# A hybrid encoder layer on one core: whole weight blocks, a router on the unnormalised sum, and a reordered end

## The reference, cut to what matters

```python
def rms_norm(x, g):
    y = x * lax.rsqrt(jnp.mean(x * x, axis=-1, keepdims=True) + RMS_EPS)
    return y * g

x = x + einsum('bsd,de->bse', y_rwkv * g, w_out)          # 512 x 1024
h = rms_norm(x, norm_ffn_g)
# expert_choice_moe: 16 experts, each takes cap = 2*512/16 = 64 tokens
logits = einsum('bsd,de->bse', h, router_w)               # 512 x 16
aff = softmax(logits, axis=-1)
gates, idx = lax.top_k(swapaxes(aff, 1, 2), cap)
xin = h[bidx, idx]
hid = silu(xin @ w_gate) * (xin @ w_up)                   # 64 x 2048 per expert
yexp = (hid @ w_down) * gates
x = x + zeros.at[bidx, idx].add(yexp)
out = rms_norm(x, final_norm_g)
```

## Time and profile before

| | before |
|---|---|
| median of 3 runs | 1600.93 us |
| profiled execution | 1600.83 us, span 1599.0 us |
| PE busy | 1461.1 us (91%) |
| DVE busy | 510.5 us (32%) |
| ACT busy | 240.1 us (15%) |
| DMA queue q1 | 479.31 MB, 78.2% of 16 engines' span |
| read from HBM | 470.83 MB |
| mean granted TensorE clock | 0.982 of full speed |

### The profile page before, as it was taken

The page is one execution under the profiler, slowest core; times in us unless marked ns, Lnnn a source line. Parts: engine busy times, 40 slices in busy tenths (PEclk is TensorE's granted clock), DMA queues, the critical chain, the costliest instruction groups (busy, mean ns, idle before and its releaser), DMA issues.

```text
span 1599.0 us, 26196 instructions
## 1 busy us (share of the span) xinstructions
PE 1461.1 (91%) x11376; PEld 735.6 (46%) x11376; DVE 510.5 (32%) x712; ACT 240.1 (15%) x478; POOL 184.5 (12%) x349
## 2 busy tenths in 40 slices
PE   7999999989888895899989989989989989989987
PEld 5344455878877653434324324324324324324322
DVE  6666534667664564101101101101101101101103
ACT  3333321222212121100000000000000000000002
POOL 1323504434333210000000000000000000000000
PEclk9999999999998997899999999999999999999999
DMA  9245577766765645499999999999999999999994
GB/s 302 66 158 185 183 264 161 176 136 133 149 111 127 263 172 210 187 428 425 421 428 422 425 427 426 425 425 427 423 426 426 425 424 428 423 425 427 422 425 184
DMA packets 186070, 500.47 MB, mean 313 GB/s; under 512 B 125904, under 2 KB 135248, under 8 KB 153216
## 3 DMA queue, kind: packets, MB, share of 16 engines
q1 hardware_dynamic: 180192, 479.31, 78.2%
q0 software_dynamic: 5792, 19.88, 3.6%
HBM read 470.83 MB, written 28.33 MB: 312 GB/s over the span
## 4 chain that ended last, share of the span: by engine, by line
PE 32%; DMA 23%; DVE 2%; issue 1%; ACT 1%; DVEq 0%; SPq 0%
DMA ring<-in_exp_w_up 23%; PE pD L1543 14%; PE pG L1504 6%; PE pU L1524 6%; PE pX L1492 4%; PE pG L1524 3%; DVE res L1652 1%; DVE hid L1670 1%; PE pX L1531 1%; ACT hidT L1613 0%; DVE res L1688 0%; ACT xin L1596 0%; PE pX L1560 0%; ACT xin L1628 0%; ACT L1631 0%
## 5 line engine op out<-in xcount | busy, mean ns | idle before, releaser
L1670 DVE TENSOR_TENSOR hid<-silu,pU 128x512 f32<-128x512 f32 x32 | 20.6, 684 | 774.5 <-PE pU L1524 774.5
L1524 PE MATMUL pU<-ring,xin 128*64 128x512 f32 x768 | 173.8, 597 | 37.8 <-DMA ring<-in_exp_w_up 37.8
L1524 PE MATMUL pG<-ring,xin 128*64 128x512 f32 x768 | 171.3, 595 | 11.4 <-DMA ring<-in_exp_w_gate 10.7
L1543 PE MATMUL pD<-ring,hidT 128*64 128x512 f32 x768 | 167.9, 593 | 2.1 <-ACT hidT L1613 2.1
L1504 PE MATMUL pG<-yexp,scatter 128*128 128x512 f32 x256 | 124.4, 618 | 3.6 <-DVE res L1652 1.9
L1524 PEld LDWEIGHTS pU<-ring,xin 128*64 128x64 f32 x768 | 52.3, 137 | 157.8 <-issue 92.0
L1524 PEld LDWEIGHTS pG<-ring,xin 128*64 128x64 f32 x768 | 53.0, 137 | 116.9 <-issue 97.6
L1543 PEld LDWEIGHTS pD<-ring,hidT 128*64 128x64 f32 x768 | 55.4, 137 | 107.7 <-issue 107.0
L1652 DVE TENSOR_TENSOR res<-res,pG 128x512 f32<-128x512 f32 x128 | 87.0, 687 | 45.9 <-PE pG L1504 45.9
L1504 PEld LDWEIGHTS pG<-yexp,scatter 128*128 128x128 f32 x256 | 40.6, 188 | 87.2 <-DVE res L1652 62.9
L1492 PEld LDWEIGHTS pX<-pick,y 128*128 128x128 f32 x512 | 59.8, 196 | 5.4 <-issue 3.4
(11 more groups left out here) (234 smaller groups left out, 1737.0 us busy)
## 6 DMA issues: line engine op xcount, KB each, us to landing
ring<-in_exp_w_gate SPq DMA_DIRECT2D x48, 2048.0 KB, 34.6
ring<-in_exp_w_up SPq DMA_DIRECT2D x48, 2048.0 KB, 27.8
ring<-in_exp_w_down SPq DMA_DIRECT2D x48, 2048.0 KB, 28.8
lent_slot<-in_exp_w_up SPq DMA_DIRECT2D x16, 2048.0 KB, 20.5
lent_slot<-in_exp_w_gate SPq DMA_DIRECT2D x16, 2048.0 KB, 31.8
lent_slot<-in_exp_w_down SPq DMA_DIRECT2D x16, 2048.0 KB, 33.8
lent_slot<-in_rw_w_in SPq DMA_DIRECT2D x8, 1024.0 KB, 12.6
scratch_sw<-tok POOLq DMA_DIRECT2D x8, 512.0 KB, 3.9
```

What stands on the lines that cost most here:

```text
L1524: mm = pe.matmul(psum[f // 2][HEAD * s:HEAD * s + HEAD, :], xin[:, k, e, :], w[:, FF * r + HALF * f:FF * r + HALF * f + HALF], start=k == ...
L1543: mm = pe.matmul(pD[h][HEAD * s:HEAD * s + HEAD, :], hidT[:, j, c, HEAD * s:HEAD * s + HEAD], w[:, 4 * half + 2 * s + c % 2, HALF * h:HALF ...
L1670: dve.tensor_tensor(hid[:, j, :], silu[:, j, :], pU[j][:, :], ALU.mult).then_inc(hid_done, 1)
```

## The change

Five edits.

1. **mix_output, router.** w_router is loaded in another order of features, in pieces of 64 B (16 numbers) where it had 512 B, and VectorE multiplies it with norm_ffn_g between first(0) and first(1) (norm_ffn_g comes by features as a row of `vec`, and by columns in a tile ffn_row). TensorE transposes the unnormalised residual, half by half as it is added, and makes the logits from that; VectorE multiplies the logits with the reciprocal root (four instructions), before the softmax. L1378 is now `normalise` and no longer in front of the logits; that of the last tile stands behind the mask copy. ScalarE squares half tiles.
2. **First gather.** Expert 0 is gathered by itself, and expert 1 behind expert 0's gate block 1.
3. **Weight blocks.** The down blocks lie in the ring so that a partition's piece is four neighbouring rows (16 KB), but for the last pair's. Blocks 4 to 15 come as halves, those loaded in the loop of pairs 1 to 6 as whole blocks of 4 MB, and the last pair's from its block 4 on as halves again. TensorE waits for both halves of a down block but in the last pair.
4. **End.** In the last pair the return of expert 14 goes between gate blocks 0 and 1 of expert 15, through pD. The last return uses four banks.
5. **Last norm.** Each tile has its own mean, root and scaling.

The core of the diff:

```diff
+def load_whole_block(sp, io, keep, expert, m, slot):
+    into = keep["ring"][slot]
+    if m < 4:
+        src, dst = up_rows(io, expert, m, 0, 4), into[:, :, :].rearrange("p (k f) d -> p k (f d)", k=4)
+    else:
+        src = down_block(io, expert, m - 4).rearrange("a (s p c) d -> p (a s) (c d)", s=2, p=P)
+        dst = into[:, :, :].rearrange("p (s c) d -> p s (c d)", s=2)
+    sp.dma_start(dst, src).then_inc(keep["landed"][slot][0], 16)
...
-            sp.dma_start(w_router[:, :, :], io["router_w"][0].rearrange("(p c) e -> p c e", p=P)).then_inc(router_load, 16)
+            sp.dma_start(w_router[:, :, :], io["router_w"][0].rearrange("(c p) e -> p c e", p=P)).then_inc(router_load, 16)
...
             def second(t):      # ScalarE
-                act.wait_ge(added, 2 * t + 2)
-                act.activation(unread, res[:, TILE_ORDER[t], :], ACT.Square, accum_out=stat[:, 0, t:t + 1]).then_inc(res_squared, 1)
-                act.wait_ge(res_mean, t + 1)
-                act.activation(stat[:, 2, t:t + 1], stat[:, 1, t:t + 1], ACT.Sqrt).then_inc(res_root, 1)
                 if t:
                     act.wait_ge(logit_mm, t)
                 for g in range(2):
+                    cols = slice(HALF * g, HALF * g + HALF)
+                    act.wait_ge(added, 2 * t + g + 1)
+                    act.activation(unread[:, cols], res[:, TILE_ORDER[t], cols], ACT.Square, accum_out=stat[:, 4 * g, t:t + 1]).then_inc(res_squared, 1)
                     act.wait_ge(turn2, 2 * t + g + 1)
-                    act.activation(h2T[:, 4 * g:4 * g + 4, :].rearrange("p c s -> p (c s)"), ps[2 + g][:, :], ACT.Copy).then_inc(turn2_ev, 1)
+                    act.activation(resT[:, 4 * g:4 * g + 4, :].rearrange("p c s -> p (c s)"), ps[2 + g][:, :], ACT.Copy).then_inc(turn2_ev, 1)
+                act.wait_ge(res_mean, t + 1)
+                act.activation(stat[:, 2, t:t + 1], stat[:, 1, t:t + 1], ACT.Sqrt).then_inc(res_root, 1)
...
                 project(t, 0)   # TensorE
                 if t:
-                    turn_h2(t - 1)
-                project(t, 1)
+                    for g in range(2):
+                        turn_res(t - 1, g)
+                if t < TILES - 1:
+                    project(t, 1)
+                else:
+                    project(t, 1, range(4))
                 if t:
                     if t == 1:
-                        pe.wait_ge(router_load, 16)
-                    logits(t - 1)
-            turn_h2(TILES - 1)
-            logits(TILES - 1)
+                        pe.wait_ge(router_scaled, 1)
+                    for g in range(2):
+                        logits(t - 1, g)
+            turn_res(TILES - 1, 0)
+            project(TILES - 1, 1, range(4, DC))
+            logits(TILES - 1, 0)
+            turn_res(TILES - 1, 1)
+            logits(TILES - 1, 1)
...
             first(0)            # VectorE
+            dve.wait_ge(router_load, 16)
+            dve.tensor_tensor(w_router[:, :, :], w_router[:, :, :], keep["vec"][:, V_FFN, :].unsqueeze(2).to_broadcast([P, DC, EXPERTS]),
+                              ALU.mult).then_inc(router_scaled, 1)
             for t in range(1, TILES):
                 first(t)
                 second(t - 1)   # waits for res_squared 2t + 2, res_root
+                normalise(t - 1)
             second(TILES - 1)
...
+            halves(0, PER + RING, False)          # SyncE, experts
+            with sp.Fori(1, PAIRS - 1) as i:
+                wholes(i)
+            halves(PAIRS - 1, PER, True)
...
+            def gather_one(g, e):                  # TensorE, experts
+                for c in range(4):
+                    k = 4 * g + c
+                    for t in range(TILES):
+                        mm = pe.matmul(pX[g][:, P * c + CAP * e:P * c + CAP * e + CAP], h2[:, t, P * k:P * k + P],
+                                       pick[:, t, e, :], start=t == 0, stop=t == TILES - 1)
+                mm.then_inc(gath_mm, 1)
...
+                    if last and e == 1:            # behind gate block 0
+                        spread(n - 1, 0, pD)
                     up_block(gate_mm, pG, 1)
+                    if first and e == 0:
+                        pe.wait_ge(scat_ev, 1 + GIVEN)
+                        for g in range(2):
+                            gather_one(g, 1)
...
-            spread(EXPERTS - 1, 1)
+            spread(EXPERTS - 1, 1, [*pG, *pU])
...
+            for t in range(TILES):                 # VectorE, the end
+                add_spread(EXPERTS - 1, last_banks, (t,))
+                if t:
+                    mean(t - 1)
+                if t > 1:
+                    scale(t - 2)
+            scale(TILES - 2)
+            mean(TILES - 1)
+            scale(TILES - 1)
```

More of the change, by code:

```diff
@@ L1510, in half_block @@
                     slot = n % RING
-                    pe.wait_ge(landed[slot][half], 16 * (TURNS * i + n // RING + 1))
+                    if half == 0:
+                        pe.wait_ge(landed[slot][0], 16 * (TURNS * i + n // RING + 1))
+                    elif first:
+                        pe.wait_ge(landed[slot][1], 16 * (n // RING + 1))
+                    elif n < RING:
+                        pe.wait_ge(landed[slot][1], 16 * (EARLY_BLOCKS // RING))
+                    elif last:
+                        pe.wait_ge(landed[slot][1], 16 * (EARLY_BLOCKS // RING + n // RING))
                     return ring[slot]
@@ L1537, in down @@
                             pe.wait_ge(down_ev, 2 * n + GIVEN)
+                            if last and e == 1:
+                                pe.wait_ge(scat_add, 2 * TILES * n + GIVEN)
+                        w = half_block(e, 4 + j, 0)
+                        if not last:
+                            half_block(e, 4 + j, 1)
                         for half in range(2):
-                            w = half_block(e, 4 + j, half)
+                            if last and half:
+                                half_block(e, 4 + j, 1)
                             for c in (2 * half, 2 * half + 1):
@@ L1542, in down @@
                                     for s in range(2):
+                                        k = 4 * half + 2 * s + c % 2 if last else 4 * s + c
                                         mm = pe.matmul(pD[h][HEAD * s:HEAD * s + HEAD, :], hidT[:, j, c, HEAD * s:HEAD * s + HEAD],
-                                                       w[:, 4 * half + 2 * s + c % 2, HALF * h:HALF * h + HALF], start=j == 0 and c == 0, stop=j == 1 and c == 3)
+                                                       w[:, k, HALF * h:HALF * h + HALF], start=j == 0 and c == 0, stop=j == 1 and c == 3)
                             mm.then_inc(down_mm, 1)
@@ L1566, in body @@
                     pe.wait_ge(silu_done, 2 * n + 2 + GIVEN)
-                    if not (first and e == 0):
-                        spread(n - 1, 1 - e)
+                    if not (first and e == 0) and not (last and e == 1):
+                        spread(n - 1, 1 - e, pG)
                     pe.wait_ge(scat_ev, n + 1 + GIVEN)
@@ L1574, in body @@
                     for j in range(2):
+                        if first and e == 0:
+                            pe.wait_ge(gath_ev, 2 + j + 1 + GIVEN)
                         if e == 1 and not last:
[L1576 removed]
+                            pe.wait_ge(gath_ev, 2 * (i + 2) + j + 1 + GIVEN)
                         turn(j)
@@ L1608, in body @@
                         act.activation(silu[:, j, :], pG[j][:, :], ACT.Silu).then_inc(silu_done, 1)
+                    if first and e == 0:
+                        gathered_one(1)
                     if e == 1 and not last:
@@ L1670, in body @@
                         dve.tensor_tensor(hid[:, j, :], silu[:, j, :], pU[j][:, :], ALU.mult).then_inc(hid_done, 1)
-                    if not (first and e == 0):
-                        add_spread(n - 1)
+                    if not (first and e == 0) and not (last and e == 1):
+                        add_spread(n - 1, pG)
             choose(0)
```

202 lines of the change are left out of this document (117 added, 85 removed).

## The result

| | before | after |
|---|---|---|
| median | 1603.31 us (4 runs, 1599.67 to 1605.77) | 1620.10 us (4 runs, 1618.09 to 1625.89) |
| profiled execution | 1600.83 us, span 1599.0 | 1625.89 us, span 1624.1 |
| mean granted clock | 0.982 | 0.964 |
| PE busy | 1461.1 us | 1484.6 us |

After against before is 1.0117, with a 95% interval of 1.0095 to 1.0140: slower. The forecast was 1610.7 us with a range of 1599 to 1620. The direction was right, and the time lies 9.4 us above the forecast, 0.1 us outside the range.

A forecast was written before the change was run, and what follows sets the result against it. The weight stream was taken as the bound: its start, length and tail make the time, and delays before the first gather count fully. Terms 20.4 - 0.2 + 1.6 - 9 - 3.1 + 0.2 = +9.9 on 1600.8: 1610.7 us, range 1599 to 1620.

The forecast's parts named there:

- Part 1: mix_output, ahead of first(1): VectorE waits for the router weights and scales them; +7.5 us (6.3 to 10).
- Part 2: mix_output, ScalarE's second(t): squares queued behind transpose copies delay VectorE; +6.2 us a step, twice, +12.3 (11 to 14).
- Part 3: mix_output: TensorE idles in three stalls and then runs at nearly the lower clock; +5.1 us (0 to 8).
- Part 4: Last tile of mix_output, to the softmax's first reduction: a shorter chain; -4.5 us (-3 to -6).
- Part 5: First gather by expert: no gain from halved columns, -0.2 us; weight stream dry for a moment, +1.6 (0 to 4).
- Part 6: Weight stream: larger pieces mean fewer piece boundaries; 9 us saved (0 to 12).
- Part 7: Expert loop: TensorE waits for whole up blocks, but slack in the pair evens it out; 0 (to +3).
- Part 8: Tail: expert 14's return moved between gate blocks, -3.1 us (-3.5 to 0); last norm +0.2 (-2 to +1).
- A: Rival, faster: the stalls in mix_output don't come, parts 1 to 3 are 0; 1585.9 us, chance 0.10.
- B: Rival, cancelled: clock falls little (1 us), first(1) takes 10.9, pieces save 12; 1601.4 us, chance 0.17.
- C: Rival: the stream isn't shortened, as pieces are cut or the engines' pace is set elsewhere; 1619.7 us, chance 0.13.
- D: Rival: the queue runs dry in the middle, whole blocks released 3.5 us late; 1621 us, chance 0.04.

The follow-up runs named there:

- late_scale: The changed kernel with VectorE's scaling of w_router moved from in front of first(1) to behind it; 1611.76 us, ratio 1.0060 to the kernel before.
- squares_first: The changed kernel with ScalarE making both squares and the root ahead of the transposed tile's copies for tiles 0 to 2; 1603.46 us, ratio 1.0005.
- both_mix: The changed kernel with the edits of late_scale and squares_first together; 1594.26 us, ratio 0.9948.
- one_gather: The changed kernel with the first gather made for both experts at once again (128 moving columns); 1612.72 us, ratio 1.0064.
- warm_expert: both_mix plus 512-column matmuls that nothing reads in TensorE's two waits ahead of the gather by expert; 1591.34 us, ratio 0.9924.
- best_split: best1 with gate and up blocks cut into pieces of 16 KB, whole 4 MB blocks kept in the middle; 1586.71 us, ratio 0.9906.
- best1: The changed kernel with the edits of late_scale, squares_first and one_gather together; 1587.73 us, ratio 0.9915.

## Why the prediction was right in direction and short in size

**What bounds the kernel** held. Every delay in front of the first gather came through at its full length, and TensorE's time in the middle, 53.7 us of 59, cost nothing.

**Part 1, router weights: mechanism right, +9.0 for +7.5.** They took 13.1 us to land, where before it was 11.8, so pieces of 64 B cost more than the 0.4 that I took, 1.3 if nothing else differed (0.9 in late_scale, where they took 12.7); L116 took 1.79 us instead of the 0.17 of the undisturbed one. The sum stays inside the bounds of part 1. late_scale takes away the whole.

**Part 2, squares behind the transposes: right.** The 12.60 us idle in front of L1407 is the queue as told, at the place that was told. Behind a turn at full clock the step is 26.1 (late_scale) for the 25.5 forecast, so the queue costs 6.8 a step where I had 6.2; squares_first brings the last step back to 19.4.

**Part 3, the clock: too small.** It cost 6.1 us where I had 5.1, inside the bound of 8: 1.2 in each of the two steps between the turns (27.3 against late_scale's 26.1 for the first, and taken to be the same for the second), and 3.7 in the last tile, by both_mix. In the steps the queue of part 2 hides some of it: the transposes and the gate took 1.97 and 3.40 instead of 1.09 and 1.88, 2.4 us more. The first two stalls are followed by 4.9 us at 0.51, here the first; behind the third the clock rose only 8.2 us after the turn, at 637.1:

```profile
574.30:579.20 4.90, 4.89 (x12) 3.12 (x13) 1.14 (x2) 1.81 (x4) 1.63 (x1) 0.51 0.85 321
```

**Part 4, last tile: right.** -4.7 at full clock in both_mix; -1.0 in after, since its stretch begins behind a stall.

**Part 5 failed, and this is the step that put the time outside the range:** "I take no gain, -0.2 for a smaller copy (between -4.5, if it went by columns, and 0)". The durations at full clock were right (7.36), and so was the dry stream. What I left out is that the gather begins at the lower clock. I had that row, 0.56 granted for 3.6 us, and used it for the stalls, but not for the changed gather itself, whose bound above I set at 0. At the lower clock a narrow instruction took nearly twice its time, 13.92 / 64 = 0.217 against 0.115, and the narrow gather didn't bring the clock back. The way from its start to the gate block became 4.8 us longer, and that from there to the first issue 2.2: 7.0 in all, where the part had -0.2. one_gather and warm_expert show it from both sides. Among the signs of the prediction, "the gather of 64 columns as long as the one of 128" did not come (13.92 against 8.90); its two signs of being wrong, the time of the first pick and the period, looked elsewhere, and neither came.

**Part 6, larger pieces: right.** A pair went from 118.3 to 116.87, 0.73 an expert; with the dry moment in it the stream is 7.8 shorter for 7.4 forecast. Of the two reasons that the price could be nothing, neither came: between 1000 and 1350 us after's 6128 data packets carry 150.7 MB, 24 KB on average, as half of them at 32 KB and half at 16 KB give, and best_split shows that the larger piece is what gains. The Trainium skill's overhead of about 3 cycles a packet (DMA: Bandwidth & Descriptors, Why small descriptors are slow), which gave 2.9 us, is too little here: an estimate from it for the 384 boundaries per engine between 16 and 32 KB in gate and up is 1.4 us, and the runs show 3.7. Its rule of 1 MiB per DMA (the same page, Rules for kernel authors) says nothing of the pieces, and the runs agree with it so far as 2 and 4 MB are alike.

**Part 7** cost nothing that shows. **Part 8** came as told: -3.4 for -2.9, and the last half of down ends the last wait.

**The sum.** Against the profile the errors are +3.5 (part 1 +1.5, part 2 +1.2, part 3 +1.0, part 4 -0.2), +7.2 (part 5), -0.4 (stream) and -0.5 (tail): 9.9 + 9.8 = 19.7, and 19.8 was measured without what lies ahead of mix_output. That the median lies only 0.1 us outside the range speaks for the width of the range and not for the working: by the traces the change costs twice what was forecast. **The rivals:** A fell, since the stalls came. Even with them taken out the same change gives 1594.26 (both_mix), not A's 1585.9: most of the 8.4 between is the gather by expert, and only best1, which gives that up too, comes near (1587.73). B and C fell with parts 3 and 6, D with the full queue in the middle: the share is 1.00 and the pairs are equally long.

Open: why the clock doesn't rise under the narrow gather. During it the weight loads are busy nearly all the time (13.73 us of 13.92), but so they are with 128 columns at the lower clock (2.00 of 2.00 in the window above), so the busy shares in these rows don't separate the two. Open as well is what moves the start of mix_output by up to 9 us from one execution to another. The clock has a part in it: one minus the granted clock, times the length, summed up to that mark in stretches of 25 us, is 6.7 us in late_scale (start at 539.1), 12.0 in after (546.1) and 12.1 in warm_expert (548.5), but also 10.5 in before (540.9), so it isn't all.

## What to carry to other kernels

Price a moved or narrowed stage at the clock that it will start with, not at that of its neighbours: behind a wait, fewer columns can take longer. Where an engine runs its queue in order, put what another engine waits for ahead of what itself waits for a third: here two squares in front of two copies were worth 16 us, and an operation on a late load in front of a loop 9. Differences below 0.3% are read between two marks inside the trace, since what lies ahead of the first mark may vary more; and a stretch of one execution is held against the same stretch of other kernels, since a fall of the clock that the code doesn't explain can sit in it (3.1 us in best1).

## What the runs showed of the hardware

- The same 64 matmuls of 128x64 took 13.92 us at a granted clock of 0.50 and 7.36 at 1.00. Behind a wait, 128 columns had the clock up after 3 to 6 us (before, one_gather, best1), 64 columns not in 13.9 us (four kernels), and 64 columns behind 3.75 us of 512-column matmuls 2 us after their start (warm_expert).
- In warm_expert the clock read 1.00 until 647 and 0.50 at 648 to 653, although 10.5 us of wide matmuls had run until 642; between lay the mask's small matmuls, 1.6 us of work in 6.4.
- Weight pieces of 8 and 16 KB gave about 421 and 426 to 428 GB/s, and gate and up in 32 KB with down in 16 KB gave 431; transfers of 2 MB and 4 MB in pieces of 16 KB were alike (117.5 and 117.46 us a pair).
- The same 64 KB of router weights, behind 2 MB of x, landed 11.8 us after the issue in pieces of 512 B (before) and 13.1 us after it in pieces of 64 B (after; 12.7 in late_scale).
